# Hybrid attention, DeltaNet and expert-retrieval layer: sample tokens loaded behind four weight chunks, the last two expert ranks gathered in halves, and a new sequence on every engine

## What is computed

```python
mod = silu(cvec) @ w_mod + b_mod                      # (1024) @ (1024, 6144); six vectors of 1024
sh_a, sc_a, g_a, sh_f, sc_f, g_f = split(mod, 6)
h = rmsnorm(x, norm_attn) * (1 + sc_a) + sh_a
da_q, da_k, da_v, dn_q, dn_k, dn_v, dn_z, dn_b, dn_a = split(h @ w_in, IN_OFFSETS)
o_da = rmsnorm(diff_attention(rope(q), [ctx_k, rope(k)], [ctx_v, v], lam), subln) * 0.8
o_dn, s_f, s_b = deltanet_mixer(dn_q, dn_k, dn_v, dn_z, dn_b, dn_a, ...)   # conv, SiLU, two directions
x = x + g_a * (concat(o_da, o_dn) @ w_out)
h = rmsnorm(x, norm_ffn) * (1 + sc_f) + sh_f
# PEER: 8 heads x top 16 of 16384 experts = 128 experts ("ranks") for each token
s = einsum('thpd,hpnd->thpn', h @ w_pq, sub_keys);  eidx, gates = product_key_top16(s)
coef = gates * gelu(sum(h * expert_u[eidx], -1))      # 128 dot products of 1024 for each token
x = x + g_f * sum(coef * expert_v[eidx])
y = rmsnorm(x, norm_out)
```

## Time and profile before

| | |
|---|---|
| time, median of 3 runs | 1343.29 us (1337.94 to 1347.5) |
| profiled execution, device time | 1348.83 us |
| its span in the profile | 1347.0 us |
| PE busy / DVE busy / ACT busy / POOL busy | 902.6 / 859.9 / 265.2 / 621.5 us |
| moved by DMA | 492.38 MB, mean 366 GB/s |
| granted TensorE clock, mean | 0.861 |

### The profile page before, as it was taken

The page is one execution under the profiler, slowest core; times in us unless marked ns, Lnnn a source line. Parts: engine busy times, 40 slices in busy tenths (PEclk is TensorE's granted clock), DMA queues, the critical chain, the costliest instruction groups (busy, mean ns, idle before and its releaser), DMA issues.

```text
span 1347.0 us, 16598 instructions
## 1 busy us (share of the span) xinstructions
PE 902.6 (67%) x5942; PEld 510.0 (38%) x5942; DVE 859.9 (64%) x2283; ACT 265.2 (20%) x704; POOL 621.5 (46%) x660
## 2 busy tenths in 40 slices
PE   5896989979859877677860166001555877777775
PEld 2754668845525565354460022000112322322222
DVE  1624328899985598926199793898007766666565
ACT  3552414431314431304000001001001002000000
POOL 0010003236577556646667777776773433333330
PEclk9897989999969988889795578555787999999999
DMA  9664457999999789899999999999999999999995
GB/s 391 249 250 189 188 203 290 346 393 330 375 388 408 294 351 406 345 374 413 385 396 410 412 410 410 410 411 390 376 412 405 427 424 426 425 425 425 423 425 210
DMA packets 102305, 492.38 MB, mean 366 GB/s; under 512 B 11344, under 2 KB 12368, under 8 KB 80848
## 3 DMA queue, kind: packets, MB, share of 16 engines
q0 software_dynamic: 92624, 404.27, 75.0%
q1 hardware_dynamic: 9600, 87.05, 16.3%
HBM read 488.65 MB, written 2.62 MB: 365 GB/s over the span
## 4 chain that ended last, share of the span: by engine, by line
PE 35%; DMA 26%; DVE 20%; POOL 8%; issue 7%; ACT 4%; SPq 0%; DVEq 0%; POOLq 0%; ACTq 0%
PE bank L1202 32%; DMA big<-in_euv,consts 11%; DVE big L2033 9%; POOL big L800 6%; DMA wring<-in_euv,consts 5%; DMA wring<-in_wch 3%; DMA big<-in_ev,rowT 2%; DVE extra L2033 2%; PE bank L1222 1%; PE bank L1208 1%; DMA big<-in_eu,idx 1%; DVE wring L2033 1%; DMA extra<-in_eu,consts 1%; POOL extra L800 1%; DMA big<-in_eu,consts 1%
## 5 line engine op out<-in xcount | busy, mean ns | idle before, releaser
L1202 PE MATMUL bank<-big,W 128*32 128x512 f32 (+1 forms) x988 | 283.1, 725 | 103.0 <-DMA big<-in_ev,rowT 44.4
L2033 DVE CUSTOM_DVE_ANT_0 big<-big,hnow 128x1024 f32<-128x1024 f32 x240 | 284.7, 1217 | 103.3 <-DMA big<-in_euv,consts 51.5
L800 POOL DMA_INDIRECT big<-in_ev,rowT x171 | 163.2, 954 | 79.1 <-issue 59.2
L1202 PEld LDWEIGHTS bank<-big,W 128*32 128x32 f32 (+1 forms) x988 | 84.6, 148 | 258.5 <-issue 248.7
L1202 PE MATMUL bank<-hT,wring 128*128 128x128 f32 (+1 forms) x1088 | 152.4, 302 | 11.0 <-ACT hT L874 6.0
L1202 PE MATMUL bank<-wring,W 128*128 128x512 f32 (+1 forms) x352 | 126.5, 648 | 46.5 <-DVE W L2056 44.9
L1202 PEld LDWEIGHTS bank<-hT,wring 128*128 128x128 f32 x1088 | 143.6, 199 | 25.1 <-issue 12.5
L2033 DVE CUSTOM_DVE_ANT_0 wring<-wring,hnow 128x1024 f32<-128x1024 f32 x64 | 77.5, 1219 | 109.4 <-DMA wring<-in_euv,consts 109.2
L810 POOL DMA_INDIRECT big<-in_euv,consts x76 | 71.3, 939 | 102.0 <-PE bank L1202 98.5
L1202 PE MATMUL bank<-big 32*32 32x32 f32 (+1 forms) x1952 | 86.5, 228 | 42.3 <-issue 10.5
L789 POOL DMA_INDIRECT big<-in_eu,consts x102 | 96.6, 947 | 37.5 <-issue 24.4
(11 more groups left out here) (318 smaller groups left out, 1395.8 us busy)
## 6 DMA issues: line engine op xcount, KB each, us to landing
wring<-in_wch SPq DMA_DIRECT2D x32, 2048.0 KB, 10.8
big<-in_wch SPq DMA_DIRECT2D x6, 1536.0 KB, 9.3
tok<-in_wch SPq DMA_DIRECT2D x6, 512.0 KB, 10.4
big<-in_ev,rowT POOLq DMA_INDIRECT x171, 8.7
big<-in_eu,consts POOLq DMA_INDIRECT x102, 10.4
xs<-in_x SPq DMA_DIRECT2D x1, 1536.0 KB, 7.4
out_y<-xs SPq DMA_DIRECT2D x3, 512.0 KB, 7.8
big<-in_euv,consts POOLq DMA_INDIRECT x76, 17.8
```

What stands on the lines that cost most here:

```text
L800: nc.gpsimd.indirect_dma_start(row(slot), None, ev, bass.IndirectOffsetOnAxis(ap=rowT[t][:, n:n + 1], axis=0)).then_inc(rows_in[slot], 16)
L1202: return nc.tensor.matmul(out, lhsT, rhs, start=first, stop=last)
L2033: V.tensor_tensor_reduce(u, u, hnow[:, :], 1.0, 0.0, ALU.mult, ALU.add, coef[t % 2][:, n:n + 1]).then_inc(dot_ready, 1)
```

## The change

1. SP loads only tile 0 of x at the start. Tiles 1 and 2, `wba` and the mask follow behind the fifth chunk in the list (after c4, when n == 4), on a semaphore of their own, `sample_in`. Whatever reads them waits for all three loads.
2. Ranks 126 and 127 of tile 2 are gathered as two U rows (`gx`) and then two V rows (`gy`) into the same places, in place of two double rows; each of them has its own `gelu` and `spread`.
3. `take.2` signals each half (`v_slot.2.127` signals its first half as well), ACT squares the halves (`half_sums`), DVE puts the sums together; the first half is scaled on DVE, the second on ACT, and each is stored by itself.
4. The sequences of all four engines are new. The number of steps is the same but for the added ones.

```diff
-            sp.dma_start(xs[:, :, :], x).then_inc(x_in, 16)
+            sp.dma_start(xs[:, 0, :], x[:, 0, :]).then_inc(x_in, 16)
             sp.dma_start(K[:, :], cst).then_inc(consts_in, 16)
-            sp.dma_start(wb[:, :, :], wba).then_inc(consts_in, 16)
-            sp.dma_start(rowT[1][:, :].bitcast(mybir.dt.uint16), msk[:, M_END:]).then_inc(consts_in, 16)
...
+                if n == 4:
+                    sp.dma_start(xs[:, 1:NT, :], x[:, 1:NT, :]).then_inc(sample_in, 16)
+                    sp.dma_start(wb[:, :, :], wba).then_inc(sample_in, 16)
+                    sp.dma_start(rowT[1][:, :].bitcast(mybir.dt.uint16), msk[:, M_END:]).then_inc(sample_in, 16)
...
+                elif t:
+                    act.wait_ge(sample_in, 48)
...
+LAST = 2
+TWOS = [(n, n + 1) for n in range(0, SLOTS - LAST, 2)] + [(n,) for n in range(SLOTS - LAST, SLOTS)]
...
+            def tail_u_rows(t, n):
+                slot, _ = row_slot(("gx", t, n))
+                row_free(("gx", t, n))
+                nc.gpsimd.indirect_dma_start(row(slot)[:, 0:D], None, eu,
...
+            def tail_v_rows(t, n):
+                slot, _ = row_slot(("gx", t, n))
+                nc.gpsimd.indirect_dma_start(row(slot)[:, D:2 * D], None, ev,
...
+            def half_sums(t):
+                for h in range(2):
+                    s = slice(512 * h, 512 * h + 512)
+                    act.wait_ge(*y_ready.at("taken", h))
+                    nc.scalar.activation(extra[:, s], xs[:, t, s], ACT.Square, accum_out=fhalf[:, h:h + 1]
...
+                if t == NT - 1:
+                    act.wait_ge(*y_ready.at("scale"))
+                    act.wait_ge(*y_ready.at("weighted", 1))
+                    nc.scalar.activation(xs[:, t, 512:D], xo[:, 0, 512:D], ACT.Copy, scale=fr)
...
+                if t == NT - 1:
+                    first, rest = xo[:, 0, 0:512], xo[:, 0, 512:D]
+                    V.tensor_tensor(first, xs[:, t, 0:512], xo[:, 1, 0:512], ALU.mult)
+                    dve.wait_ge(*fin_out.at("sum", 0))
+                    link(V.tensor_scalar(fss, fhalf[:, 0:1], 1.0 / D, EPS, ALU.mult, ALU.add))
+                    dve.wait_ge(*fin_out.at("sum", 1))
+                    V.scalar_tensor_tensor(out=fss, in0=fhalf[:, 1:2], scalar=1.0 / D, in1=fss, op0=ALU.mult, op1=ALU.add)
+                    V.tensor_tensor(rest, xs[:, t, 512:D], xo[:, 1, 512:D], ALU.mult)
...
+                    V.tensor_scalar(xs[:, t, 0:512], first, fr, None, ALU.mult)
```

Of the sequences, the places that the prediction speaks of:

```diff
 PE
-x_turn.0.0 mod.0 x_turn.0.1 mod_turn.0 mod.1 mod_turn.1 mod.2 mod_turn.2 x_turn.0.2 mod.3 mod_turn.3 channels.0.0
+mod.0 mod_turn.0 mod.1 mod_turn.1 mod.2 x_turn.0.0:2 mod_turn.2 mod.3 mod_turn.3 x_turn.0.2 channels.0.0 channels.1.0
...
-token.0.0 c_turn.7.0 c_turn.8.0 gate_in gate_rest c_turn.9.0 c_turn.10.0 token.1.0 c_turn.11.0 token.2.0 decay
-da_turn.0 qk_turn.0 dn_decay.0.0:2 mod.4 dn_scores.0.0:2 mod.5 token.3.0 dn_p.0.0.1 dn_p.0.1.1 score.0.0 dn_t.0.0.1
+token.0.0 c_turn.8.0 c_turn.9.0 gate_in gate_rest token.1.0 c_turn.10.0 c_turn.11.0 decay da_turn.0 qk_turn.0
+dn_decay.0.0:2 dn_scores.0.0 token.2.0 dn_scores.0.1 token.3.0 dn_p.0.1.1 score.0.0 dn_p.0.0.1 dn_t.0.1.1 mod.4
+dn_t.0.0.1 dn_p.0.1.2 score.0.1 dn_p.0.0.2 mod.5 dn_t.0.1.2 dn_t.0.0.2 dn_p.0.1.3 dn_p.0.0.3 dn_t.0.0.3 a_turn.0.0
...
 DVE
-norm.0.0:2 mod_turn.0 norm.0.2 mod_turn.1:4 scales.0 modulate channels.0.0 channels.1.0 channels.2.0 lam channels.3.0
+mod_turn.0:2 norm.0.0:3 lam mod_turn.2:4 scales.0 modulate channels.0.0 channels.1.0 channels.2.0 channels.3.0
...
-dot.1.118:128 coef.1.1 places.2.1.1 dot.2.0:2 chosen.2.1.1.0 dot.2.2 slot_gates.2.0 dot.2.3 last_norm.0 take.1
-spread.0:2 dot.2.4:6 spread.2
+slot_gates.1.1 dot.1.105:116 experts.2.0.1 dot.1.116:128 coef.1.1 dot.2.0:4 slot_gates.2.0 take.1 spread.0
+chosen.2.1.0.0 spread.1 dot.2.4:6 spread.2
...
 ACT
-norm.0.0 x_copy.0.0 norm.0.1 x_copy.0.1 mod.0:2 norm.0.2 mod.2 x_copy.0.2 mod.3 modulate channels.0.0 channels.1.0
+mod.0:3 norm.0.0 x_copy.0.0 norm.0.1 x_copy.0.1 norm.0.2 lam mod.3 modulate x_copy.0.2 channels.0.0 channels.1.0
...
-s_copy.2.2 s_copy.3.1 fill.1.0.2 fill.1.0.1 q_copy.3.2 ... fill.1.1.0 places.2.1.1 places.2.0.0 h_load.2 fill.1.1.1
+s_copy.3.1 coef.1.0 fill.1.0.1 s_copy.2.2 fill.1.0.0 fill.1.0.3 ... fill.1.1.0 fill.1.1.2 h_load.2 fill.1.1.1 fill.1.1.3
```

More of the change, by code:

```diff
@@ L226 @@
-channels.4.1 channels.5.1 top_key.1.0 channels.6.1 channels.7.1 pair_sums.0.0.1 channels.8.1 top_pair.0.0.1 dot.0.0:2
-channels.9.1 dot.0.2:6 channels.10.1 channels.11.1 places.0.0.1 chosen.0.0.1.0 key_norm chosen.0.0.1.1 key_scale.2
-experts.0.0.1 top_key.2.0 dot.0.6:9 dn_scale.2.1 expert_rows.0.0 dot.0.9:11 mod_turn.11 dot.0.11 dn_decay.2.1
-dot.0.12:15 dn_scores.2.1 dn_p.2.1.0 dot.0.15 top_key.3.0 pair_sums.0.1.1 rope.1.0 dn_p.2.1.1 key_scale.1 dot.0.16
-dn_p.2.1.2 dn_tt.2.1.1 dot.0.17 dn_qg.2.1 dot.0.18:20 dn_tt.2.1.2 dot.0.20:22 dn_p.2.1.3 dot.0.22:25 slot_gates.0.0
@@ L266 @@
-spread.57 dot.2.116:118 spread.58 dot.2.118:120 spread.59 dot.2.120:122 spread.60 dot.2.122:124 spread.61
-dot.2.124:126 spread.62 dot.2.126:128 spread.63 take.2 last_norm.2
+decay dn_scale.0.0:2 dn_decay.0.0:2 dn_scores.0.0:2 dn_p.0.0.0 dn_p.0.1.0:2 dn_tt.0.1.1 expo.0.0 dn_p.0.0.1 diff.0.0
+dn_tt.0.0.1 expo.0.1 dn_p.0.1.2 diff.0.1 dn_p.0.0.2:4 dn_tt.0.0.2 dn_p.0.1.3 dn_tt.0.1.2 dn_tt.0.0.3 dn_p.0.0.4
+dn_full.0.0 dn_p.0.1.4 dn_tt.0.1.3 dn_p.0.0.5 dn_full.0.1 dn_p.0.1.5 mod_turn.5 expo.0.2:4 dn_p.0.0.6 diff.0.2:4
@@ new lines @@
+dn_scale.2.1 dot.0.6:10 expert_rows.0.0 mod_turn.11 dot.0.10:12 dn_decay.2.1 dn_qg.2.1 dot.0.12 dn_scores.2.1
+dn_p.2.1.0 dot.0.13 key_scale.1 dot.0.14 dn_scale.1.0 top_key.3.0 dn_p.2.1.1 rope.1.0 dn_p.2.1.2 pair_sums.0.1.1
+dn_tt.2.1.1 dot.0.15:18 dn_tt.2.1.2 dn_p.2.1.3 dot.0.18:26 dn_p.2.1.4 dot.0.26 dn_tt.2.1.3 dot.0.27:30 slot_gates.0.0
+dot.0.30 dn_full.2.1 dn_p.2.1.5 dot.0.31:37 dn_p.2.1.6 dot.0.37:43 top_pair.0.1.0 dot.0.43:52 dn_o.2.1 dn_s.2.1
+dot.0.52:54 rope.2.1 dot.0.54:57 dn_scale.1.1 dot.0.57:60 dn_decay.1.0 dot.0.60 places.0.1.0 dot.0.61:64 coef.0.0
@@ new lines @@
+c_turn.9.0 gate_copy silu.11.0 gate_in c_turn.10.0 token.1.0 c_turn.11.0 decay da_turn.0 qk_turn.0 dn_decay.0.0:2
+token.2.0 token.3.0 dn_t.0.1.1 expo.0.0 dn_t.0.0.1 diff.0.0 expo.0.1 dn_t.0.1.2 dn_t.0.0.2:4 mod.5 a_copy.0.0
+dn_t.0.1.3 v_copy.0.0 diff.0.1 a_copy.0.1 v_copy.0.1 dn_t.0.0.5 dn_t.0.1.5 expo.0.2:4 diff.0.2 a_copy.0.2 dn_t.0.0.6
+dn_t.0.1.6 v_copy.0.2 diff.0.3 dn_v.0.0:2 a_copy.0.3 v_copy.0.3 head_norm.0.0:2 gate.0.0.0 o_copy.0 gate.0.0.1 mod.9
+norm.1.0 x_copy.1.0 q_copy.0.0 s_copy.0.0 q_copy.1.0 s_copy.1.0 channels.0.1 channels.1.1 silu.0.1 channels.2.1
```

293 lines of the change are left out of this document (165 added, 128 removed).

## The result

| | before | after |
|---|---|---|
| median of 4 runs | 1342.32 us (1337.94 to 1347.5) | 1364.11 us (1362.1 to 1367.67) |
| profiled execution, its span | 1348.83, 1347.0 | 1362.1, 1360.3 |

The ratio is 1.0164 with a 95% interval of 1.012 to 1.0208: the changed kernel is slower by 22 us (16 to 28), clear of no change. The forecast was 1344.9 with a range up to 1359. The two profiled executions lie 13.3 apart, since the one of before is 6.5 above its median.

What follows compares the result with a forecast made beforehand. DMA near its limit from about 600 us, before that the chain to the first gathers, and a chain at the end were taken as the bound. Terms +9.4 -3.8 +0.5 -0.8 -1.3 -2.4 = +1.6 gave 1344.9 us, range 1329 to 1359.

Steps and rivals of the forecast that it cites:

- Part 1, +9.4: Start: tile 0's steps wait behind late x, so channels.0.0 starts at 48.6, not 39.21 us; +9.4, bounds +7.9 to +10.5.
- x comes early: Rival, start: loads overtake each other, x is there at about 25 us, start 3 us faster, total 1332.5; chance 0.05.
- Tile 0, -3.8 + 0.5 - 0.8: Up to first gather: two mods leave a full PE -3.8, run later +0.5, mod_turn.9 fills a wait -0.8; gather +5.3 late.
- The middle, 0: 200 to 1000 us: reordered steps taken as 0, with -9.5 to +9.5 from DMA dips closed or opened.
- the term's +9.5: Middle, 200 to 1000 us: upper end, if as much DMA time is lost as closing half the dips would gain.
- Start of tile 2 and end, -1.3 - 2.4: last_norm.0 moved from before take.1 removes a DMA dip, -1.3; last ranks and stores in halves shorten the end, -2.4.
- Premise: "whatever delays the first gathers delays the end by as much": Whole run: DMA is near its limit from about 600 us, so earlier delays of the first gathers reach the end in full.
- Forecast +1.6: Whole kernel: sum of +9.4 -3.8 +0.5 -0.8 -1.3 -2.4, on a span of 1347.0 us; as median 1344.9.
- Carried whole: Rival: start delay reaches the end, moved mods cost +3.8, token.2.0 gains nothing; 1352 us, 1353 at upper end; chance 0.20.
- middle worse: Rival, 200 to 1000 us: DMA loses time there, one more refill costs 9.2, giving 1354 us, two 1363; chance 0.10.

Runs made afterwards that it cites:

- e7: Kernel before with the new tail and new PE, DVE and ACT lists for tile 0 only (channels.0.0 to query.0.0): -0.5 us (-3.5 to 2.4) against before.
- e8: Kernel before with the new tail and all new PE, DVE and ACT lists from query.0.0 on, POOL's list old: +15.7 us (11.4 to 20.0) against before.
- middle 2: The lists of PE, DVE and ACT from coef.0.1 on (about 560 us); new alone, with the new tail: +1.3 us against the kernel before.
- e6: Kernel before with the new tail and new lists only from coef.0.1 on (about 560 us): +1.3 us (-2.0 to 4.7) against before.
- middle 1: The lists of PE, DVE and ACT from query.0.0 to coef.0.1 (about 200 to 560 us); new alone, with the new tail: +7.4 us against before.
- e12: Kernel before with the new tail and new lists only from query.0.0 to coef.0.0 (200 to 365 us): +3.4 us (-0.7 to 7.4) against before.
- e10: Kernel before with the new tail and the new start alone (late x, new lists up to channels.0.0): +12.0 us (7.4 to 16.5) against before.
- e5: Kernel before with the new tail and new lists only from query.0.0 to coef.0.1 (about 200 to 560 us): +7.4 us (4.7 to 10.1) against before.
- e17: e8 with resid.2.1, gate.1.0.1 and norm.1.2 moved back behind coef.0.1: +17.2 us (13.0 to 21.5) against the kernel before.
- e9: Changed kernel with resid.2.1, gate.1.0.1 and norm.1.2 moved back behind coef.0.1: +17.1 us (11.6 to 22.6) against the kernel before.
- e4: Kernel before with the new tail and late x, its readers moved behind tile 0's first steps: -1.1 us (-5.4 to 3.3) against before, slow chip.

## Why the prediction was wrong

- **Part 1, +9.4: right.** `channels.0.0` at 49.40, +10.2 (bounds 7.9 to 10.5); c0 at 11.6, predicted 12.0; x at 33.6, predicted 34.9; `x_turn.0.1` 37.0, predicted 37.5; `mod.3` 3.51, predicted 3.5. "x comes early" fell: the load took 11.7 us behind the chunks. That agrees with the Trainium skill, DMA: Bandwidth & Descriptors, "Queues, rings and completion order", by which descriptors are consumed in ring order. (The rival's "behind 3 MB" was misread: at 422 GB/s the 8.9 us of c4 are 3.8 MB with its own 2.1, so 1.7 MB stood ahead.)
- **Tile 0, -3.8 + 0.5 - 0.8: wrong by 4 to 5.** From the end of the wait for c7 (57.30 before, 67.78 after) to the first `dn_p` it is 53.0 before and 53.4 after. The step took PE as full and took out the mods. But `token.2.0` and `token.3.0` now stand in series where DVE's matrices are awaited, with waits of 1.25, 1.12 and 1.00 left between, and the four groups of matmuls from `decay` on ran slower (1.98, 1.95, 1.91 and 3.10 instead of 1.40, 1.07, 1.04 and 1.95), at a granted clock of 0.62 from 94 to 103 us where it was 1.00 before. The mods behind were free: from there to `norm.1.0`'s transposes it is 50.9 against 51.2. e7's time, -0.5, fits. So the first gather was 11.0 late and not 5.3.
- **The middle, 0: the step that failed.** It cost 15.7 alone (e8), more than the term's +9.5. I put the parts' worth at "no row shows what a swap is worth", and looked for DMA dips to close. The list shows what I left uncounted: between `coef.0.1` and `v_batch.0.1.12`, the last batch that PE does before `gu.1.0` is issued (it starts at 652.99 and 678.67, `gu.1.0` comes at 660.21 and 682.17), stand 320 matmuls of queries and not 192 (`query.1.2`, `query.2.1` and their rests moved past it). At 7.4 us for 64 that is 14.8 us more on a PE that was 77% busy in that stretch, with POOL waiting for the batches' places (34.8 us of long waits and not 18.9); the traces show 125 matmuls and 14.3 us more. That is one part of the 15.7, not the whole: the exchange was not run alone, and with the rest of middle 2 it costs 1.3 or 8.3, by what stands ahead of it (e6 has the 638 matmuls and 108.5 us too, and loses nothing clear of noise). The other part is middle 1, 7.4 alone; which of its exchanges costs that stays open, and so does why the two together cost 15.7.
- **Start of tile 2 and end, -1.3 - 2.4: right in sign, -2.6 instead of -3.7 in the trace.** From the first double row to the end 343.8 became 341.2 and 341.3. With the tail and the old lists it is 341.8 to 343.3 (e12, e10, e5, e7), with the new lists 341.1 to 342.6 (e17, e9), so the two terms can't be told apart. The two runs of the tail alone, +0.5 and +0.1, can't tell this from nothing. The table load takes 1.28 us, of which 1.05 are in the open (DVE's sum is there at 1354.84), and the root follows at 1355.89, 0.02 behind it. The Trainium skill, ScalarE: Activation LUTs, "What ACT_TABLE_LOAD costs", adds a drain of 1.38 us to a switch; this trace shows none. (For "the next instruction right behind it" I gave, where ACT's next instruction starts only at 1342.32; the rows of the changed kernel's end are the ones that show it.)
- **Premise: "whatever delays the first gathers delays the end by as much".** True with the old middle (e10: 12.7 late, +12.0). With the new one about 5 of 11, by differences that are 6 us uncertain.
- **Sum.** Forecast +1.6. By parts, each with the new tail in it: start +12.0, tile 0 -0.5, middle +15.7, which is 27.2; measured 20.2 and 22.0, so 5 to 7 are given back where the parts meet by these figures, an amount that is itself uncertain by about 8 (POOL's new list is in it as well, and was not run alone). "Carried whole" (0.20) and "middle worse" (0.10) both happened, together; each was priced alone, at most 1363, and I didn't price them as one.

## What to carry to other kernels

Don't put a reordering at zero by default: for each step that frees a buffer another queue waits for, count the work of that engine ahead of it in the old list and in the new one, in us, and price the difference where that engine has little idle time (PE was 77% busy here). It is a price with a range: the same shift cost 1.3 us behind the old middle 1, where DMA stayed at 395 GB/s, and 8.3 behind the new one. Where loads come late, only what stands behind their first reader in an in-order list pays; x could come late for nothing (e4) with the readers moved back. Losses need not add: here two parts of the middle came out dearer together than apart (15.7 and 8.7), start and middle cheaper (20.2 and 22.0 for 27.2), each just at the edge of what the runs can tell. So measure the parts alone and together.
